# A decoder block on one core: the router reads raw sums, the gather reads x1 regrouped by chunk, and alpha*x1 is added behind the first round

## What is computed

```python
x = layer_norm(alpha * x + mix, ln1_g[l], ln1_b[l])
ffn = hierarchical_moe(x, w_router_group[l], w_router_expert[l], w_gate[l], w_up[l], w_down[l])
x = layer_norm(alpha * x + ffn, ln2_g[l], ln2_b[l])
...
g_prob = softmax(xt @ w_router_group); g_top_p, g_top = top_k(g_prob, 1)
e_logits = (xt @ w_router_expert).reshape(-1, N_GROUPS, EXPERTS_PER_GROUP)
e_top_logit, e_top = top_k(e_in_group, EXPERT_TOPK)
h = silu(xt @ w_gate) * (xt @ w_up) * combine      # 32 experts, 256 wide
out = h @ w_down
```

## Time and profile before

| | |
|---|---|
| median of 3 runs | 451.51 us (449.73 to 452.6) |
| the profiled execution, its own time | 448.62 us |
| its span | 446.9 us |
| PE busy | 407.0 us, 91% |
| PEld busy | 307.3 us, 69% |
| DVE / ACT / POOL busy | 158.4 / 120.0 / 15.0 us |
| moved by DMA | 134.66 MB, mean 301 GB/s |

### The profile page before, as it was taken

The page is one execution under the profiler, slowest core; times in us unless marked ns, Lnnn a source line. Parts: engine busy times, 40 slices in busy tenths (PEclk is TensorE's granted clock), DMA queues, the critical chain, the costliest instruction groups (busy, mean ns, idle before and its releaser), DMA issues.

```text
span 446.9 us, 6921 instructions
## 1 busy us (share of the span) xinstructions
PE 407.0 (91%) x2741; PEld 307.3 (69%) x2742; DVE 158.4 (35%) x307; ACT 120.0 (27%) x198; POOL 15.0 (3%) x37
## 2 busy tenths in 40 slices
PE   7899899999999999897999779799898798999997
PEld 6799898987999999784647327355373273645647
DVE  3444578773555564478211001001101011011116
ACT  4344454562644444130311001001110010111010
POOL 2000000000000000122000000000000000000004
PEclk9999999999999999998899979988999699999999
DMA  8899866638476767976069999999999999997802
GB/s 283 223 337 352 302 214 226 246 95 280 134 261 197 261 198 263 402 303 243 1 241 428 420 422 420 422 422 420 406 429 422 422 422 420 422 422 279 300 1 94
DMA packets 54499, 134.66 MB, mean 301 GB/s; under 512 B 6608, under 2 KB 39376, under 8 KB 42704
## 3 DMA queue, kind: packets, MB, share of 16 engines
q1 hardware_dynamic: 53904, 132.29, 78.0%
q0 software_dynamic: 576, 2.10, 1.4%
HBM read 133.33 MB, written 1.05 MB: 301 GB/s over the span
## 4 chain that ended last, share of the span: by engine, by line
PE 53%; DMA 28%; DVE 8%; SPq 4%; ACT 3%; issue 2%; POOL 0%; ACTq 0%; DVEq 0%
DMA dn<-in_w_down 27%; PE bank L927 21%; PE bank L1168 8%; PE bank L1119 7%; PE bank L1141 5%; PE bank L1044 5%; PE bank L1021 3%; PE bank L1175 2%; SPq L347 2%; PE bank L935 2%; DVE wl L636 2%; SPq L320 1%; DMA raw<-in_w_in 1%; ACT wh L493 1%; DVE x L765 1%
## 5 line engine op out<-in xcount | busy, mean ns | idle before, releaser
L636 DVE TENSOR_TENSOR wl<-raw,wh 128x1024 fp32r<-128x1024 f32 x56 | 68.3, 1224 | 68.2 <-ACT wh L493 67.9
L927 PE MATMUL bank<-xh,wh 128*128 128x256 f32 x288 | 82.9, 288 | 3.3 <-DVE wl L636 1.7
L927 PE MATMUL bank<-xl,wh 128*128 128x256 f32 x288 | 81.4, 283 | 0.0
L927 PE MATMUL bank<-xh,wl 128*128 128x256 f32 x288 | 81.4, 283 | 0.0
L493 ACT ACTIVATE wh<-raw 128x1024 fp32r<-128x1024 f32 x56 | 58.7, 1055 | 66.1 <-PE bank L927 32.7
L1119 PEld LDWEIGHTS bank<-pick,x 128*128 128x128 f32 x288 | 70.0, 335 | 4.2 <-issue 1.9
L1119 PE MATMUL bank<-pick,x 128*128 128x128 f32 x288 | 69.2, 401 | 1.3 <-DVE pick L816 1.3
L1141 PE MATMUL bank<-gu,xg 128*32 128x512 f32 x512 | 58.2, 607 | 7.3 <-issue 7.3
L927 PEld LDWEIGHTS bank<-xh,wh 128*128 128x128 f32 x288 | 55.1, 191 | 6.1 <-issue 3.8
L927 PEld LDWEIGHTS bank<-xl,wh 128*128 128x128 f32 x288 | 55.2, 192 | 0.2 <-issue 0.2
L927 PEld LDWEIGHTS bank<-xh,wl 128*128 128x128 f32 x288 | 55.2, 192 | 0.0
(11 more groups left out here) (182 smaller groups left out, 411.9 us busy)
## 6 DMA issues: line engine op xcount, KB each, us to landing
gu<-in_w_gate SPq DMA_DIRECT2D x32, 1024.0 KB, 10.8
gu<-in_w_up SPq DMA_DIRECT2D x32, 1024.0 KB, 12.8
dn<-in_w_down SPq DMA_DIRECT2D x28, 1024.0 KB, 19.0
raw<-in_w_in SPq DMA_DIRECT2D x40, 512.0 KB, 4.8
raw<-in_w_o SPq DMA_DIRECT2D x8, 512.0 KB, 4.8
dn<-in_w_down SPq DMA_DIRECT2D x8, 512.0 KB, 8.1
raw<-in_w_out_conv SPq DMA_DIRECT2D x4, 512.0 KB, 3.5
raw<-in_w_out_attn SPq DMA_DIRECT2D x4, 512.0 KB, 4.5
```

The costliest lines, as they stand in the source:

```text
L636: dve.tensor_tensor(wl[:, s, :].rearrange("p (k c) -> p k c", k=KC), raw[:, pair % NRAW, :].rearrange("p (k c) -> p k c", k=KC) [:, :, n % ...
L927: mm = pe.matmul(dst, w[:, k, :], v[:, i, :], start=(i == 0 and w is h and v is high_in), stop=(i == len(ks) - 1 and w is l))
```

## The change

x1 holds the raw z first, copied from the banks by ScalarE as each half is finished: the last `merge` goes half by half and signals `acc_done` four times. Moments are taken from this copy, and transposes start on it without waiting for the moments. The logits are corrected by VectorE: `rstd * (z @ (g*w)) - mean*rstd * sum(g*w) + sum(b*w)`; the two sums come from one product of 72 columns that now stands ahead of the last two merges. Of the four evacuations of the transposes the last is VectorE's. Behind them ScalarE writes the normed rows, without gain and bias, into a new tile `x1p` as (chunk, column) with each chunk contiguous. The gather reads `x1p`; gain and bias (per partition there) come in as `xg` is evacuated, four instructions of 128 columns on either engine instead of one of 512. ScalarE does the routing's exponential ahead of its part of the first evacuation. The gate/up product waits for `xg_v` only at chunk 4. The real x1 is made by VectorE in four passes, one ahead of `take_gathered(1)`, three behind `weigh_slots(1, 0)`; alpha*x1 is seeded after quad 0's rounds over banks that four bf16 products with zeros have cleared. All 8 quads are written out, with one read of `bounds` for each.

```diff
@@ scalar
-            act.wait_ge(shift_done, 1)
-            for h in range(2):
-                act.activation(x1[:, 0, h * HALF:(h + 1) * HALF], bank[h][:, :], ACT.Identity,
-                               scale=rstd[:, 0:1], bias=shift[:, 0:1]).then_inc(norm_done[0], 1)
+            for t in range(TT):
+                for h in range(2):
+                    act.wait_ge(acc_done, 2 * t + h + 1)
+                    act.activation(x1[:, t, h * HALF:(h + 1) * HALF], bank[2 * t + h][:, :],
+                                   ACT.Copy).then_inc(z_sb[t], 1)
...
+            act.wait_ge(neg_mean_done, 1)
+            for t in range(TT):
+                act.wait_ge(z_sb[t], 2)
+                act.activation(x1p[:, t, :, :], x1[:, t, :].rearrange("q (p k) -> q k p", k=KC), ACT.Identity,
+                               scale=rstd[:, t:t + 1], bias=neg_mean[:, t:t + 1]).then_inc(x1p_done, 1)
...
-                act.activation(xg[:, 0:KC // 2, :], bank[4][:, :].rearrange("p (k s) -> p k s", s=P),
-                               ACT.Copy).then_inc(xg_a, 1)
+                for k in range(KC // 2):
+                    ins = act.activation(xg[:, k, :], bank[4][:, k * P:(k + 1) * P], ACT.Identity,
+                                         scale=gcol[:, k:k + 1], bias=bcol[:, k:k + 1])
+                ins.then_inc(xg_a, 1)
@@ vector
+            for t in range(TT):
+                ins = dve.scalar_tensor_tensor(offs[:, t, :], rsum_b[:, 0:NL], neg_mean[:, t:t + 1],
+                                               rsum_b[:, NL:2 * NL], ALU.mult, ALU.add)
...
+            for t in range(TT):
+                ins = dve.scalar_tensor_tensor(logit[:, t, :], bank[4][:, t * NL:(t + 1) * NL],
+                                               rstd[:, t:t + 1], offs[:, t, :], ALU.mult, ALU.add)
...
-                dve.tensor_copy(xg[:, KC // 2:KC, :],
-                                bank[5][:, :].rearrange("p (k s) -> p k s", s=P)).then_inc(xg_v, 1)
+                for k in range(KC // 2, KC):
+                    ins = dve.tensor_scalar(xg[:, k, :], bank[5][:, k % 4 * P:(k % 4 + 1) * P],
+                                            gcol[:, k:k + 1], bcol[:, k:k + 1], ALU.mult, ALU.add)
+                ins.then_inc(xg_v, 1)
+            def scale(t):
+                return dve.scalar_tensor_tensor(x1[:, t, :], x1[:, t, :], moments[:, t, 0:1], lng[:, :],
+                                                ALU.subtract, ALU.mult)
+            def shift_rows(t):
+                dve.scalar_tensor_tensor(x1[:, t, :], x1[:, t, :], rstd[:, t:t + 1], lnb[:, :],
+                                         ALU.mult, ALU.add).then_inc(x1_done, 1)
@@ tensor
+            pe.wait_ge(moment_done, TT)
+            for b in range(2 * TT):
+                pe.matmul(bank[b][:, :], zeros_b[:, :],
+                          zeros_b[:, :].unsqueeze(1).to_broadcast([P, HALF // P, P]),
+                          start=True, stop=True, skip_group_check=True)
...
-                        mm = pe.matmul(bank[4 + k // 4][:, (k % 4) * P:(k % 4 + 1) * P], x1[:, t, k::KC],
+                        mm = pe.matmul(bank[4 + k // 4][:, (k % 4) * P:(k % 4 + 1) * P], x1p[:, t, k, :],
...
                         pe.wait_ge(xg_a, c + 1)
-                        pe.wait_ge(xg_v, c + 1)
                         pe.wait_ge(bank_free[6], c + 1)
                         pe.wait_ge(gu_in[half], 2 * QE * 16 * loads)
                         for k in range(KC):
+                            if k == KC // 2:
+                                pe.wait_ge(xg_v, c + 1)
...
-            with pe.Fori(0, NQ // 2 - 1) as o:
-                for half in range(2):
-                    quad(2 * o + half, half, o + 1, False)
-            for half in range(2):
-                quad(NQ - 2 + half, half, NQ // 2, half == 1)
+            begin = 0
+            for q in range(NQ):
+                begin = quad(q, begin, q % 2, q // 2 + 1, q == NQ - 1)
+                if q == 0:
+                    pe.wait_ge(x1_done, X1_PARTS)
+                    seed(True)
```

More of the change, by code:

```diff
@@ L225, in hybrid_block @@
         shift_done = sem("shift_done")
-        norm_done = [sem(f"norm_done{t}") for t in range(TT)]
+        z_sb = [sem(f"z_sb{t}") for t in range(TT)]
+        neg_mean_done = sem("neg_mean_done")
+        x1p_done = sem("x1p_done")
         acc_done = sem("acc_done")
@@ L754, in _ @@
                 variance(t)
+            dve.wait_ge(x1T_ps, 4)
+            dve.tensor_copy(x1T[:, KC // 2:KC, P:2 * P],
+                            bank[7][:, :].rearrange("p (k s) -> p k s", s=P)).then_inc(bank_free[7], 1)
             dve.wait_ge(rstd_done, 2)
-            for h in range(2):
-                dve.tensor_scalar(x1[:, 1, h * HALF:(h + 1) * HALF], bank[2 + h][:, :], moments[:, 1, 0:1],
-                                  rstd[:, 1:2], ALU.subtract, ALU.mult).then_inc(norm_done[1], 1)
@@ L760, in _ @@
-            dve.wait_ge(bias_ps, 1)
-            dve.tensor_copy(rbias[:, :], bank[6][:, 0:NL]).then_inc(bias_read, 1)
-            dve.wait_ge(ln_in, 32)
-            for t, cols in ((0, slice(0, DM)), (1, slice(0, HALF))):
-                dve.wait_ge(x1T_ps, 2 * t + 2)
-                link(dve.tensor_tensor(x1[:, t, cols], x1[:, t, cols], lng[:, cols], ALU.mult))
-                dve.tensor_tensor(x1[:, t, cols], x1[:, t, cols], lnb[:, cols],
-                                  ALU.add).then_inc(x1_done, 1)
+            dve.scalar_tensor_tensor(neg_mean[:, :], moments[:, :, 0], -1.0, rstd[:, :],
+                                     ALU.mult, ALU.mult).then_inc(neg_mean_done, 1)
@@ L881, in _ @@
             weigh_slots(1, 0)
+            shift_rows(0)
+            link(scale(1))
+            shift_rows(1)
             dve.wait_ge(rounds_done, 1)
@@ L929, in product, with seed @@
                 return mm
-            def seed(signal):
+            def seed(over_zeros):
                 for t in range(TT):
@@ L1033, in branches, with merge @@
                 product(bank[6 + m][:, SEQ:2 * SEQ], U0 + m, range(CC, KC), oh, ol).then_inc(unit_done, 1)
-            def merge(j, m, at, in_loop=True):
+            def merge(j, m, at, final=False):
                 n = U0 + at + m
@@ L1046, in merge @@
                                            start=False, stop=True, skip_group_check=True)
-                    if m == 1 and not in_loop:
-                        mm.then_inc(acc_done, 1)
-                if in_loop or m == 0:
+                        if final:
+                            mm.then_inc(acc_done, 1)
+                if not final:
                     mm.then_inc(unit_done, 1)
@@ L1066, in _ @@
                 branches(JP - 1, m)
-            for m in range(2):
-                merge(JP - 1, m, 2, False)
-            pe.wait_ge(y_done, KC)
+            pe.wait_ge(sig_done, 2 * JP)
             pe.wait_ge(wrb_done, 1)
             for k in range(KC):
-                mm = pe.matmul(bank[6][:, 0:NL], ones[:, :], wrb[:, k, :],
+                mm = pe.matmul(bank[4][:, 0:2 * NL], ones[:, :], wr[:, k, :],
                                start=(k == 0), stop=(k == KC - 1))
             mm.then_inc(bias_ps, 1)
+            for m in range(2):
+                merge(JP - 1, m, 2, m == 1)
             def transpose_tile(t):
-                pe.wait_ge(norm_done[t], 2)
+                pe.wait_ge(z_sb[t], 2)
                 for k in range(KC):
@@ L1125, in _, with quad @@
             pe.wait_ge(rank_read, 1)
+            pe.wait_ge(x1p_done, TT)
             gather(0)
             pe.wait_ge(rounds_done, 1)
-            def quad(q, half, loads, in_columns):
+            def quad(q, first, half, loads, in_columns):
                     w = gu[half]
-                    first = pe.value_load(bounds[0:1, bass.ds(q, 1)], min_val=0, max_val=MAX_ROUNDS)
-                    end = pe.value_load(bounds[0:1, bass.ds(q + 1, 1)], min_val=1, max_val=MAX_ROUNDS)
+                    end = pe.value_load(bounds[0:1, q + 1:q + 2], min_val=1, max_val=MAX_ROUNDS)
                     with pe.Fori(first, end) as c:
                         pe.wait_ge(xg_a, c + 1)
-                        pe.wait_ge(xg_v, c + 1)
                         pe.wait_ge(bank_free[6], c + 1)
```

106 lines of the change are left out of this document (57 added, 49 removed).

## The result

The changed kernel takes 437.06 us (median of 4 runs, 436.24 to 438.32) against 452.06 (449.73 to 453.02) for the kernel before, timed with it: ratio 0.9691, interval 0.9658 to 0.9724. That is 3.1% faster, as forecast (438, 431 to 446). The profiled executions moved less: 448.62 to 436.95, and the span from 446.9 to 435.2.

The account below looks back on a forecast made before the run. Bound by the weight stream (152.9 us) and the engine work before and after it. Terms: -6.7 ahead, stream unchanged, -6.9 behind, together -13.6: 448.62 to 435.0, plus 2.9 for a median, 438; range 431 to 446.

Parts of the forecast that it names:

- What bounds the kernel: Whole span: before, during and after the 152.9 us expert weight stream; engines can shorten only the first and last parts.
- The router: Last merge to logits and routing: logits taken at 199.7 instead of 203.59, -3.9 us; routing chain kept at 6.9.
- The gather: TensorE's gather in each round: contiguous x1p cuts it to 3.8 us; gather start to gate/up start becomes 4.1.
- The clock: TensorE after pauses: lower clock costs 1.9 us at the first gather and 1.9 at the stream's end.
- x1p and memory lines: ScalarE's two passes to x1p: reading with a 32-byte step might double them, until 203.2, still hidden.
- The rest of x1: VectorE's four passes and the seed: h of round 0 1.7 us late, seed 3.6, both hidden by the stream.
- The stream: Expert weights, quad 2's issue to landing of quad 5's down weights: pure transfer of 152.9 us, length unchanged.
- The stream keeps its 152.9: Step of the sum: the weight stream starts earlier by 6.7 us but stays 152.9 us long.
- a stream longer than 153: Weight stream: a length over 153 us was named beforehand as showing the prediction wrong.
- the forecast of the median: Whole kernel: 435.0 us for a profiled execution, plus 2.9 for a median, so 438, given 55%.
- my term of +1.9 "once at the stream's end": Round 5's down product, ending the stream: a longer pause lowers the clock, charged 1.9 us once.

Follow-up runs that it names:

- e8_transposes_after_moments: Changed kernel, but the transposes of z wait for the moments of both tiles; 440.72 us, ratio to the kernel before 0.9772.
- e2_gather_strided: Changed kernel, but x1p is kept in the order of x1 and the gather reads it with the step of 8 words; 447.31 us, ratio 0.9919.
- e6_xgv_at_start: Changed kernel, but the gate/up product waits for VectorE's half of xg at its start again, not at chunk 4; 441.56 us, ratio 0.9778.
- a_again: The changed kernel once more, unchanged, as the measure for runs beside it; 437.10 us, ratio to the kernel before 0.9697.
- e1_ln_late: Changed kernel, with the second norm's gain and bias fetched only when the last down weights' first half has landed; 434.72 us, ratio 0.9628.
- e9_before_ln_late: Kernel before the change, with only the second norm's gain and bias fetched behind the last down weights; 450.90 us, ratio 0.9971.

## Why the prediction was right, and where it was not

**What bounds the kernel: right.** The three parts behaved as three parts. What TensorE saved inside the stream went into its pauses (7.91 instead of 1.82 before round 5's down product). I had forecast some 6.2 there: the gather and its gap gave 4.9, and 1.05 came from round 4's down product, which took 5.24 instead of 6.29.

**The router: right, a little undersized.** Logits were taken at 199.52; forecast 199.7. The last merge ended at 194.07, not near 193.6; but the mixer's last branch product had ended 0.7 later too (186.71 against 185.99), and from there to the merge's end both kernels take 7.36. So the moved bias product cost nothing where I charged 0.2, and the rest is how this execution of the mixer ran. The routing step, kept at 6.9, was 6.31. Before, the five products of the ranks stood in TensorE's queue behind a seed that ran to 209.1 (granted clock 0.50 from 205 to 208), while `chosen` was ready at 208.3; now TensorE waits for `chosen` (3.99 idle before 204.27). I had kept the whole chain and not looked at what its one TensorE step was queued behind. e8_transposes_after_moments shows that the absence of a wait is worth 3.4 to 3.9 as this kernel stands, of which I had reckoned with the wait's 2.2 and not with the clock's share. No run undoes VectorE's part alone (normalisation, gain and bias taken out of its way to the logits), so how the 4.07 divide between the two stays open.

**The gather: right.** 3.8 forecast, 3.73 measured; gather to product 4.1 forecast, 388.24 - 384.58 = 3.66 measured, since ScalarE's four pieces overlap more than I allowed (four took 1.50). VectorE's ended 1.6 behind the gather as forecast, and the moved wait hides them. The order of x1p and the moved wait carry this part, as e2_gather_strided (10 us) and e6_xgv_at_start (4.5 us) show.

**The clock: right in kind and size.** 1.9 was charged at each place; 5.26 - 3.73 = 1.5 and 5.63 - 3.64 = 2.0 were paid in the profiled execution, and 1.4 to 2.7 at the first gather in the runs that leave it as it is (5.16 to 6.41 long). In the changed kernel's trace the granted clock is 0.50 when the down product behind the 7.91 starts:

```profile
375.50:376.50 1.00, 1.00 (x8) 0.37 (x12) 0.00 (x0) 0.00 (x0) 0.00 (x0) 0.50 1.02 426
```

The rule of the Trainium skill ("TensorE: Matmul & The Clock Gate", section "HAM oscillation — how this bites in real kernels") that each burst behind a pause for transfers starts cold held in all ten pauses of over 5 us of the traces of the changed kernel and a_again: the granted clock was 0.50 at the start of each of those down products. What I missed is that the kernel before also ran a product at the lower level behind a gather and a gap of only 0.92. Its gate/up product of round 3 took 8.67 instead of 7.07 (its timeline row, and one us of it with the granted clock third from the end):

```profile
307.39 8.67 PE L1141 MATMUL bank<-gu,xg 128*32 128x512 f32 x64 [0.92 <-issue]
...
308.30:309.30 1.00, 1.00 (x12) 0.35 (x8) 0.28 (x2) 0.00 (x0) 0.00 (x0) 0.50 1.04 434
```

So the length of the pause alone does not tell where the clock is low.

**x1p and memory lines: right.** ScalarE's passes doubled (1.23 to 2.2 each), and were hidden, until 201.3 against 205.8. The rule of the Trainium skill ("SBUF — State Buffer", section "Door 1: The DMA port swizzle") that each new 16-byte line pays agrees with the gather's weight loads and with ScalarE's passes. It does not agree with the transposes, which read x1 with the same step: 16 of them take 2.02 in the changed kernel, 0.12 each. So here the step cost two kinds of instruction and not a third; why is not shown.

**The rest of x1: right.** VectorE's passes (1.27 to 1.28) made h late by 1.4, where 1.7 was forecast (gate/up to down product 11.0 in round 0, 9.6 in round 6), and the pause before its transpose is 1.57. Seed and passes together were covered, with 9.41 of pause left before round 1's down product. Of that, 3.6 come from the longer stream; without it 5.76 are left (e1_ln_late), against some 5.0 by my figures.

**The stream: wrong.** "The stream keeps its 152.9" is the step that failed; it was 157.18, and a stream longer than 153 was one of my own signs of being wrong. I went through SyncE's queue and past GpSimd's: the sum has no line for what GpSimd issues when `x1_done` is complete, though the change moved that from 203.96 to 218.5, from queues about to run empty into the stream's start. 1.05 MB at 420 GB/s is 2.5 us; it cost 3.6 (e1_ln_late), all of it before the first down weights of the stream land (36.99 us from quad 2's issue to round 1's down product, 33.34 in e1_ln_late, 33.58 before). Some 0.7 of stretching is left even then (153.5 to 153.6 against 152.9) and I did not find its cause.

**Why the forecast of the median still came out.** In part by luck. For the profiled execution I had forecast 435.0, and it took 436.95, some 2 more. For the median I added 2.9, the distance in the kernel before; in the changed kernel it is 0.1 (437.06 and 436.95). The two errors go against each other and leave 438 only 0.9 off. In differences, the terms gave -13.6, the profiled executions -11.7, the medians -15.0. The two ends were 2.4 better than forecast and the stream 4.3 worse, which is the -11.7. The rest lies in the kernel before: in the execution that I read, round 5's pause was 1.82 and its down product at full pace. In the trace of e9_before_ln_late, the same program up to there, it is this, with round 4's down product above it:

```profile
350.70 3.64 PE L1169 MATMUL bank<-dn,hT 128*32 128x512 f32 x32 [1.13 <-DMA dn<-in_w_down]
...
380.51 6.31 PE L1169 MATMUL bank<-dn,hT 128*32 128x512 f32 x32 [4.46 <-DMA dn<-in_w_down]
```

The weights land at the same distances from quad 2's issue in both traces (123.1 and 152.9). What differs is which product is slow: in the kernel before, round 4's (6.29), which made round 5's pause 2.6 shorter; here round 4's runs at full pace, round 5's pause is 4.46, and its product pays 2.7 for the clock where no stream covers it. The part behind the stream is 70.1 instead of 67.4. The execution that I had read was the luckier one of the two, and my term of +1.9 "once at the stream's end" was partly paid in the median before. One such trace is not a distribution; how often it happens was not measured.

## What to carry to other kernels

When a signal is moved, list everything that waits for it on every engine, the transfers above all: two small fetches on GpSimd's queue, free before in an empty stretch of the queues, cost 3.6 of the 16 us won at the two ends as soon as they met the weight stream. Follow each engine's queue of transfers, not only that of the engine that issues most of them. Put the step of an access on the side that has time: here ScalarE pays it once, hidden, instead of TensorE's weight loads in each round. And look at the granted clock behind each wait of TensorE that stands on the path: where it has fallen, the wait costs its length and the slower instructions too (2.2 and 1.6 in e8_transposes_after_moments). In two other pauses a few unused products got 1.5 and 2.0 us back.

## What I had not expected of the hardware

A pause of only 2.16 us brought the granted clock to 0.55 to 0.60 behind it (e8_transposes_after_moments), while 1.82 before 379.47 in the kernel before brought none and a gap of 0.92 behind a gather stood before the slow gate/up product at 307.39. The broadcast fetch of 1.05 MB cost the stream 3.6 us, 1.4 times its share by bytes, and took 9.5 and 12.7 us from issue to landing. Reading f32 with a step of 32 bytes cost TensorE's weight loads (334 ns instead of 199 a load) and ScalarE (2226 ns instead of 1232 for 1024 columns) about the same factor, 1.7 to 1.8; the gather as a whole took twice as long (7.64 instead of 3.73), while the transposes with the same step kept their pace.
